# Dilated attention on one core: the scores of two heads issued as a pair, one PSUM bank for the filler product

## The reference, cut to what matters

```python
def dilated_attention(q, k, v):
    b, h, s, hd = q.shape
    outs, lses = [], []
    for window, dil in DILATED_PATTERNS:
        def split(t):
            return t.reshape(b, h, s // dil, dil, hd).swapaxes(2, 3)
        o, lse = banded_causal_attention(split(q), split(k), split(v), window // dil)
        outs.append(o.swapaxes(2, 3).reshape(b, h, s, hd))
        lses.append(lse.swapaxes(2, 3).reshape(b, h, s))
    w = jax.nn.softmax(jnp.stack(lses), axis=0)
    return jnp.einsum('pbhs,pbhsd->bhsd', w, jnp.stack(outs))
...
    y_a = o_a.transpose(0, 2, 1, 3).reshape(b, s, ATTN_WIDTH_3).astype(x.dtype) * jax.nn.silu(za)
```

## Time and profile before

| what | value |
|---|---|
| median of 3 runs | 4103.49 us (4103.43 to 4115.32) |
| the profiled execution, its time | 4107.38 us |
| its span, first to last instruction | 4105.6 us |
| TensorE busy over the span | 3791.0 us (92%) |
| VectorE busy | 2193.6 us (53%) |
| ScalarE busy | 958.7 us (23%) |
| granted TensorE clock, mean | 0.956 |

### The profile page before, as it was taken

How to read it: one execution, slowest core, us unless ns; L and a number is a source line. 1 busy time by engine, 2 the same in 40 slices (tenths; PEclk the granted TensorE clock), 3 DMA queues, 4 the chain that set the end, 5 groups by cost and what they waited for, 6 DMA issues and landing times. The chain is left out here.

```text
span 4105.6 us, 43463 instructions
## 1 busy us (share of the span) xinstructions
PE 3791.0 (92%) x17243; PEld 2989.3 (73%) x17243; DVE 2193.6 (53%) x2909; ACT 958.7 (23%) x1898; POOL 406.0 (10%) x172
## 2 busy tenths in 40 slices
PE   8999879999998969976879999996999999989998
PEld 6665568888886758866658888885777777767487
DVE  6565466655658373989564443446222223346294
ACT  1455410000002151133240000004012222232362
POOL 0112113323321001323000000000000000000000
PEclk9998789999999889999889999998999999999999
DMA  4100112222222111110111111113111212142122
GB/s 153 32 21 21 52 57 91 75 90 100 75 104 89 56 64 42 41 52 21 36 62 50 52 41 61 41 62 114 41 46 57 72 53 71 42 179 83 66 63 77
DMA packets 137322, 267.54 MB, mean 65 GB/s; under 512 B 11648, under 2 KB 42452, under 8 KB 137172
## 3 DMA queue, kind: packets, MB, share of 16 engines
q1 hardware_dynamic: 137172, 265.48, 18.2%
HBM read 220.38 MB, written 45.09 MB: 65 GB/s over the span
## 5 line engine op out<-in xcount | busy, mean ns | idle before, releaser
L130 PE MATMUL banks<-region_parts 128*128 128x512 f32 x3290 | 1312.3, 399 | 95.8 <-DVE weight_chunks_parts L124 85.2
L132 PE MATMUL banks<-region_parts,weight_chunks_parts 128*128 128x512 f32 x2112 | 828.0, 392 | 0.0
L130 PEld LDWEIGHTS banks<-region_parts 128*128 128x128 f32 x3290 | 623.4, 189 | 270.3 <-issue 87.1
L131 PE MATMUL banks<-weight_chunks_parts,region_parts 128*128 128x512 f32 x1984 | 778.1, 392 | 0.0
L131 PE MATMUL banks<-region_parts 128*128 128x512 f32 x1658 | 649.4, 392 | 0.0
L132 PE MATMUL banks<-region_parts 128*128 128x512 f32 x1632 | 639.7, 392 | 0.0
L132 PEld LDWEIGHTS banks<-region_parts,weight_chunks_parts 128*128 128x128 f32 x2112 | 399.8, 189 | 85.6
L131 PEld LDWEIGHTS banks<-weight_chunks_parts,region_parts 128*128 128x128 f32 x1984 | 376.4, 190 | 81.8 <-issue 5.4
L554 ACT ACTIVATE region<-gain_offset 128x512 f32<-128x512 f32 x128 | 81.0, 633 | 1270.9 <-DVE gain_offset L502 1270.9
L131 PEld LDWEIGHTS banks<-region_parts 128*128 128x128 f32 x1658 | 314.0, 189 | 65.3 <-issue 2.4
L132 PEld LDWEIGHTS banks<-region_parts 128*128 128x128 f32 x1632 | 309.0, 189 | 65.4
(11 more groups left out here) (390 smaller groups left out, 4975.7 us busy)
## 6 DMA issues: line engine op xcount, KB each, us to landing
weight_chunks<-in_w_in SPq DMA_DIRECT2D x19, 2048.0 KB, 8.1
weight_chunks<-in_w_up SPq DMA_DIRECT2D x16, 2048.0 KB, 8.5
weight_chunks<-in_w_down SPq DMA_DIRECT2D x16, 2048.0 KB, 7.7
extra<-in_w_ada SPq DMA_DIRECT2D x16, 1536.0 KB, 10.8
x_spill<-region SPq DMA_DIRECT2D x32, 512.0 KB, 10.8
weight_chunks<-in_w_out SPq DMA_DIRECT2D x8, 2048.0 KB, 8.4
region<-x_spill SPq DMA_DIRECT2D x32, 512.0 KB, 6.0
f_spill<-region SPq DMA_DIRECT2D x64, 256.0 KB, 2.0
```

The source lines that it names most:

```text
L130: pe.matmul(out, m.parts(lhs[0]), m.parts(rhs[0]), start=first, stop=False)
L131: pe.matmul(out, m.parts(lhs[0]), m.parts(rhs[1]), start=False, stop=False)
L132: return pe.matmul(out, m.parts(lhs[1]), m.parts(rhs[0]), start=False, stop=last)
```

## The change

Scores are issued for two units at once, on even n, as pairs of products: for each block of up to 512 columns first the even head on rows 0-63, then the odd head on rows 64-127. They go to four banks, 0 and 1 for the even head, 2 and 3 for the odd. The transposed weights move to banks 4 and 5, the result to bank 6, and the filler has bank 7 alone, so that group n now waits for group n-1 to be taken out. The result's turn stays in bank 5, which it shares with the second half of the weights' turn: `turn` of a unit with t of 4 or more gets a wait for `gate`, `turn_out` gets a wait for ScalarE's copies of the turn before it, and it stands behind `out` in the iteration. The orders of ScalarE and VectorE do not change.

```diff
@@ dilated_attention
+    OUT_BANK, FILL_BANK = 6, 7
@@ tensor
             def scores(n):
                 h, t = units[n]
-                b, w = 64 * (h % 2), (t + 1) * P
+                w = (t + 1) * P
                 if n >= 1:
                     pe.wait_ge(max_ready, n)
                 for lo in range(0, w, HALF):
                     hi = min(w, lo + HALF)
-                    mm = pe.matmul(m.bank[:, lo // HALF, 0:hi - lo], q[b:b + 64, h // 2, t * P:(t + 1) * P],
-                                   k[b:b + 64, h // 2, lo:hi], start=True, stop=True)
-                mm.then_inc(s_done, 1)
+                    for odd in range(2):
+                        b = 64 * odd
+                        mm = pe.matmul(m.bank[:, 2 * odd + lo // HALF, 0:hi - lo], q[b:b + 64, h // 2, t * P:(t + 1) * P],
+                                       k[b:b + 64, h // 2, lo:hi], start=True, stop=True)
+                        if hi == w:
+                            mm.then_inc(s_done, 1)
             def turn(n):
                 h, t = units[n]
                 pe.wait_ge(exp_ready, n + 1)
+                if n >= 4 and halves(t) == 2:
+                    pe.wait_ge(y_ready, n // 2 - 1)
...
-                        mm = pe.transpose(m.bank[:, 2 + g, (j % 4) * P:(j % 4 + 1) * P],
+                        mm = pe.transpose(m.bank[:, 4 + g, (j % 4) * P:(j % 4 + 1) * P],
...
             def turn_out(g):
                 pe.wait_ge(rows_ready, 2 * g + 2)
+                pe.wait_ge(copied, turns[min(2 * g + 3, N - 1)])
                 if g:
                     pe.wait_ge(y_ready, g)
                 pe.transpose(m.bank[:, 5, 0:P], o_rows[g % 2], m.ident).then_inc(o_turned, 1)
             for n in range(N + 3):
-                if n < N:
+                if n < N and n % 2 == 0:
                     scores(n)
                 if n < NG:
                     pe_filler(pe, m, F, n // 8, n % 8)
                 if 1 <= n <= N:
                     turn(n - 1)
+                if 2 <= n < N + 2:
+                    out(n - 2)
                 if n >= 4 and n % 2 == 0:
                     turn_out(n // 2 - 2)
-                if 2 <= n < N + 2:
-                    out(n - 2)
@@ vector
-                src = m.bank[:, 0:2, :].rearrange("p b n -> p (b n)")[:, 0:w]
+                src = m.bank[:, 2 * (n % 2):2 * (n % 2) + 2, :].rearrange("p b n -> p (b n)")[:, 0:w]
@@ pe_filler
-    if n >= 2:
-        pe.wait_ge(wt.bank_free, NBANK + F.base + n - 1)
+    if n >= 1:
+        pe.wait_ge(wt.bank_free, NBANK + F.base + n)
...
-        mm = split_products(m, pe, m.bank[:, 6 + n % 2, :], w, v, k == 0, k == NK - 1)
+        mm = split_products(m, pe, m.bank[:, 7, :], w, v, k == 0, k == NK - 1)
```

More of the change, by code:

```diff
@@ L1573, in out @@
                 for j in range(t + 1):
-                    mm = pe.matmul(m.bank[:, 4, 0:64], PT[n % 2][:, j * P:(j + 1) * P], va[:, j, h * 64:(h + 1) * 64],
+                    mm = pe.matmul(m.bank[:, OUT_BANK, 0:64], PT[n % 2][:, j * P:(j + 1) * P], va[:, j, h * 64:(h + 1) * 64],
                                    start=(j == 0), stop=(j == t))
@@ L1610, in _ @@
                     if n >= SILU:
-                        act.activation(stage[n % 2], m.bank[:, 6 + n % 2, :], ACT.Tanh, scale=0.5).then_inc(half_open, 1)
+                        act.activation(stage[n % 2], m.bank[:, FILL_BANK, :], ACT.Tanh, scale=0.5).then_inc(half_open, 1)
                     else:
                         if n >= GATE:
-                            ins = act.activation(stage[n % 2], m.bank[:, 6 + n % 2, :], ACT.Tanh, scale=0.5)
+                            ins = act.activation(stage[n % 2], m.bank[:, FILL_BANK, :], ACT.Tanh, scale=0.5)
                         else:
-                            ins = act.activation(stage[n % 2], m.bank[:, 6 + n % 2, :], ACT.Copy)
+                            ins = act.activation(stage[n % 2], m.bank[:, FILL_BANK, :], ACT.Copy)
                         ins.then_inc(staged, 1)
@@ L1627, in _ @@
                         act.wait_ge(turned, (turns[u - 1] if u else 0) + g + 1)
-                        act.activation(PT[u % 2][:, g * HALF:g * HALF + w], m.bank[:, 2 + g, 0:w], ACT.Copy).then_inc(copied, 1)
+                        act.activation(PT[u % 2][:, g * HALF:g * HALF + w], m.bank[:, 4 + g, 0:w], ACT.Copy).then_inc(copied, 1)
             for i in range(MEM_T):
@@ L1664, in rows @@
                 dve.wait_ge(o_done, n + 1)
-                dve.tensor_scalar(o_rows[n // 2 % 2][:, 64 * (n % 2):64 * (n % 2) + 64], m.bank[:, 4, 0:64], x[:, 3:4], None,
+                dve.tensor_scalar(o_rows[n // 2 % 2][:, 64 * (n % 2):64 * (n % 2) + 64], m.bank[:, OUT_BANK, 0:64], x[:, 3:4], None,
                                   ALU.mult).then_inc(rows_ready, 1)
@@ L1675, in silu @@
                 dve.wait_ge(half_open, n - SILU + 1)
-                dve.scalar_tensor_tensor(stage[n % 2], stage[n % 2], 1.0, m.bank[:, 6 + n % 2, :], op0=ALU.add,
+                dve.scalar_tensor_tensor(stage[n % 2], stage[n % 2], 1.0, m.bank[:, FILL_BANK, :], op0=ALU.add,
                                          op1=ALU.mult).then_inc(staged, 1)
```

## The result

| what | before | changed |
|---|---|---|
| median | 4103.31 us (20 runs) | 4115.66 us (20 runs) |
| lowest and highest run | 4098.06 to 4115.48 | 4106.22 to 4126.06 |
| ratio to before | | 1.0027, 95% interval 1.0019 to 1.0035 |
| profiled execution, its time and span | 4107.38, 4105.6 | 4115.48, 4113.1 |
| the stage, from its first score product to the next stage's first product | 538.7 | 547.1 |

The change costs 12 us in the medians; the ratio, worked out over all runs, says 0.27%. Forecast were +8.3 us. The sum was good; two of its terms were not, and their errors cancelled.

A forecast was written before the change was run, and what follows sets the result against it. TensorE was taken to bound the stage, with no waits. Terms: −9.0 − 19.7 + 7.6 + 1.3 + 26.5 + 1.6 = +8.3 us, 4111.8 us against the 4103.5 median; range 4100 to 4131.

The forecast's parts named there:

- term 5: Filler groups 49 to 63: waits for DVE to free the one bank, after logits and silu; 26.5 us lost.
- Term 2: Score visits: paired products on the two row halves overlap as far as in-order records allow; 19.7 us gained.
- terms 1 and 2: Score visits: 64 become 32, 9.0 us gained; overlap of the paired heads' products, 19.7 us gained.
- rival C: Score pairs: halves run two by two, a pair costing as much as one head; −8, 4104 us; chance 0.08.
- Term 6: TensorE's clock in this stage: new idle time brings one fall to 1.2 GHz; 1.6 us lost.
- Rival B: Fifteen waits of 1.3 to 2.5 us: the clock falls at every one; +24 − 1.6, 4134 us; chance 0.08.
- Term 3: Result's turn on even n from 4: waits for ACT's copies of the turn before; 7.6 us lost.
- Term 4: Filler groups 1 to 47: waits for the one bank, only at the first groups; 1.3 us lost.

The follow-up runs named there:

- experiment 1: Changed kernel with silu(n-1) moved ahead of rows(n-3) and logits(n) in VectorE's list: 4075.5 us, ratio 0.9924 to the kernel before.
- experiment 4: Kernel before with only the filler's single bank 7, group n waiting for group n-1: 4149.3 us, ratio 1.0106.
- experiment 3: Changed kernel with the pair undone, each unit's scores issued in its own iteration in the same four banks: 4161.37 us, ratio 1.0138 to the kernel before.
- experiment 7: Changed kernel with the pair's loops swapped, all even-head score products before the odd head's: 4113.64 us, ratio 1.0016 to the kernel before.
- experiment 6: Changed kernel plus six unread products ahead of the filler's bank wait on odd n from 49 to 63: 4107.29 us, ratio 0.9999 to the kernel before.
- experiment 9: Kernel before with one filler bank and silu moved ahead in VectorE's list: 4100.98 us, ratio 0.9989.

## Why the prediction was right, and where it was not

**Right in sum and in sign of each term.** +8.3 us were forecast, the stage grew by 8.4, the median by 12.4, inside the range. Whether it is "no change that counts" is less clear: the prediction set that limit at 12.3 us, and the result stands right at it. The largest loss was found where it was put: term 5, fifteen waits for VectorE's release in groups 49 to 63. 26.5 us were forecast with the last head pair's turns inside; measured are 28.1 us, or 29.9 with those turns. Experiments 1 and 4 show it from both sides. Its shape is as worked out too: at t = 7 the chain from the first score product to the filler was 4.15 us (3586.46 to 3590.61), against 1.91 + 0.26 + 2.02 = 4.2.

**Term 2 was mis-sized.** The step that failed is "TensorE takes records in order", which gave five slots of eight, and 28.7 us for terms 1 and 2 together. Measured are 42.1 us by the records, 40.3 by experiment 3. The price of a pair is that of one head, at t = 7 four slots in place of five, as rival C had it with a chance of 0.08. Experiment 7 shows what is wrong in the step: with all of the even head's products issued first, each of the odd head's still starts 0.013 us behind its counterpart. The two row halves took their products independently of each other here. The rule cited from the Trainium skill beside term 2 (TensorE: Matmul & The Clock Gate, Part 3), that products on different row groups run concurrently a few nanoseconds apart, is what the trace shows (0.006 to 0.007 us), and in fuller measure than I drew from it; its second half, starts in program order across row groups, does not hold in experiment 7.

**Term 6 was mis-sized.** One fall of the clock was allowed, 1.6 us. The profiled execution has seven, each a drop to 1.2 GHz that makes a filler group about 6.95 us long from its first product to its last instead of 5.35. That is 1.6 us each, 11 us in all; all filler groups together grew by 10.2. (The prediction got its 1.6 from 6.9 and 5.6, which are measured to different ends; the size is right all the same.) Group 62 first, with the fall, then group 63, without:

```profile
3590.60:3597.60 7.00, 6.99 (x24) 5.63 (x25) 3.61 (x9) 0.58 (x2) 0.00 (x0) 0.76 0.10 37
3602.60:3608.20 5.60, 5.55 (x24) 4.57 (x25) 0.36 (x2) 0.62 (x2) 0.00 (x0) 1.00 0.14 50
```

I had let one row decide, 2.6 us idle in 7 at full clock, and had counted only the waits above 2.2 us. But the length of a wait does not tell whether the clock falls: the seven falls followed waits of 1.7 to 2.4 us (groups 49, 54, 55, 57, 60, 61 and 62), while groups 58, 59 and 63, with waits of 2.0 to 2.6 us, did not fall. The number of waits should have gone into the term, not the longest ones. That they are the cause is shown by experiment 1 (the waits all but gone, no falls) and by experiment 6, where the groups whose wait was filled did not fall. Rival B was half true: seven of fifteen. The Trainium skill's section cited beside B (same page, A second HAM failure mode), on a clock that keeps falling and rising when the engine idles between groups, fits this kernel, with seven falls in fifteen waits.

**Term 3 was near.** 7.6 us forecast for the first three head pairs, 8.7 us measured. Over all four it is 10.5; the last pair's share, 1.8 us, stood in term 5. **Term 4**: 1.3 us forecast, 1.7 measured.

So 13 us too little gained and 9 us too little lost to the clock, with 5 us more of waits (40.3 against 35.4 in terms 3 to 5): the errors cancel. What was right by reasoning is the waits; that the total is within 4 us of the measured one is partly luck. With the visits sized right and the rest as forecast, the same sum would have come to 5 us faster than before.

## What to carry to other kernels

When two consumers or stages share a resource that had two buffers and gets one, read what stands ahead of the release in the releasing engine's list: here one buffer cost 45 us with the release behind `logits` (experiment 4) and nothing that could be measured with it ahead (experiment 9). The change as a whole was sound and only lacked that line: with `silu` moved it is 0.76% faster than the kernel before, and with the result's turn inside the filler group as well, 1.03% faster. Two float32 products with a contraction of 64, on rows 0-63 and 64-127 into different banks, cost as much here as one.

## What the runs showed of the hardware that I had not expected

- Products on the two row halves ran with no loss at all: 1.92 us for two heads of 1024 columns against 1.91 for one, and the order in which they were issued did not matter (1.93 us in experiment 7).
- A wait of TensorE costs more than its length. In experiment 4, 27.6 us of waits brought 18.1 us of slower products; in the changed kernel 29.8 brought 10.2. Filling eight of the fifteen waits with products that nothing reads made the kernel faster (experiment 6).
